# Hymba-style layer on one core: the small score and gate products move behind the near scores, in quadrants

## The reference, cut to what matters

```
proj = rmsnorm(x) @ w_in            # 1024 x 3072: sb q, k, v, gate; lru x, gate; xa q, gate
SB : stick-breaking attention, 8 heads x 64, strictly causal
     w = sigmoid(z) * prod of (1 - sigmoid(z)) over the later keys; out = w @ v
LRU: xc = width-4 causal convolution of lru_x
     r, i = sigmoid(xc_block @ w_rg + b_rg), sigmoid(xc_block @ w_ig + b_ig)   # 4 blocks of 64
     h = scan(exp(-8 r softplus(-lam)), sqrt(1 - a^2) * i * xc)
XA : softmax attention, 4 heads x 64, into 256 memory tokens
out = x + concat(sb*silu(gate), h*silu(gate), xa*silu(gate)) @ w_out
```

## Time and profile before

| | us |
|---|---|
| median of 3 runs (1554.22 to 1555.98) | 1555.12 |
| span of the profiled execution | 1551.8 |
| the runs' median over the span | 3.3 |
| TensorE busy | 1506.0 (97%) |
| VectorE busy | 1040.6 (67%) |
| ScalarE busy | 878.3 (57%) |
| GpSimd busy | 318.3 (21%) |

### The profile page before, as it was taken

One profiled execution on the slowest core, in us unless ns is written; L12 is line 12 of the kernel. 1 busy time (PEld: TensorE's weight loads), 2 busy tenths in 40 slices (PEclk: granted clock), 3 DMA queues, 4 the chain that ended last, 5 costly groups with the idle time before them and its releaser, 6 DMA issues.

```text
span 1551.8 us, 29770 instructions
## 1 busy us (share of the span) xinstructions
PE 1506.0 (97%) x10764; PEld 732.2 (47%) x10764; DVE 1040.6 (67%) x1907; ACT 878.3 (57%) x1593; POOL 318.3 (21%) x305
## 2 busy tenths in 40 slices
PE   4999999999999999999999999999999999999996
PEld 2444444444444444444444444444444444444452
DVE  6988766676666676666666665667666667666674
ACT  6887555565446565445566445566545556544661
POOL 3222111222211222212222211222211122221120
PEclk9999999999999999999999999999999999999998
DMA  9545665545655545555545556454555454565645
GB/s 364 197 126 103 155 131 111 118 115 133 145 124 120 119 116 126 142 122 128 130 105 122 138 125 145 109 117 114 134 140 131 115 118 116 128 145 123 124 95 137
DMA packets 443336, 205.83 MB, mean 133 GB/s; under 512 B 412000, under 2 KB 412448, under 8 KB 442144
## 3 DMA queue, kind: packets, MB, share of 16 engines
q1 hardware_dynamic: 443008, 205.18, 54.8%
q10 hardware_dynamic: 288, 0.13, 0.0%
HBM read 55.53 MB, written 50.53 MB: 68 GB/s over the span
## 4 chain that ended last, share of the span: by engine, by line
PE 85%; SPq 2%; ACT 2%; DMA 1%; issue 1%; DVE 1%; ACTq 0%; DVEq 0%
PE bank L1816 26%; PE bank L1818 25%; PE bank L1817 25%; PE bank L1900 2%; SPq L495 2%; PE bank L2014 2%; PE bank L1864 2%; PE bank L1885 1%; PE bank L1909 1%; DMA x_lo<-x_t 0%; PE bank L1953 0%; PE bank L1948 0%; PE bank L1950 0%; PE bank L1949 0%; ACT fail_and_take L1047 0%
## 5 line engine op out<-in xcount | busy, mean ns | idle before, releaser
L1816 PE MATMUL bank<-w_pair,x_hi 128*128 128x512 f16 x1528 | 581.6, 381 | 9.4 <-DVE w_pair L1248 5.2
L1818 PE MATMUL bank<-w_pair,x_lo 128*128 128x512 f16 x1528 | 580.6, 380 | 0.0
L1817 PE MATMUL bank<-w_pair,x_hi 128*128 128x512 f16 x1528 | 580.5, 380 | 0.0
L1143 ACT ACTIVATE spare<-xy,columns 128x1024 f16<-128x1024 f32 x32 | 36.8, 1149 | 395.4 <-DVE columns L1674 395.4
L1816 PEld LDWEIGHTS bank<-w_pair,x_hi 128*128 128x128 f16 x1528 | 149.7, 98 | 183.4 <-issue 6.9
L1818 PEld LDWEIGHTS bank<-w_pair,x_lo 128*128 128x128 f16 x1528 | 149.8, 98 | 181.4 <-issue 1.9
L1817 PEld LDWEIGHTS bank<-w_pair,x_hi 128*128 128x128 f16 x1528 | 149.9, 98 | 166.8 <-issue 2.7
L1816 PE MATMUL bank<-wo_pair,y_hi 128*128 128x512 f16 x480 | 181.9, 379 | 0.8 <-issue 0.8
L752 POOL TENSOR_TENSOR fail_and_take<-fail_and_take,seen 128x512 f32<-128x512 f32 x32 | 42.5, 1327 | 680.9 <-ACT fail_and_take L904 680.9
L1817 PE MATMUL bank<-wo_pair,y_hi 128*128 128x512 f16 x480 | 181.9, 379 | 0.0
L1818 PE MATMUL bank<-wo_pair,y_lo 128*128 128x512 f16 x480 | 181.9, 379 | 0.0
(11 more groups left out here) (271 smaller groups left out, 2398.3 us busy)
## 6 DMA issues: line engine op xcount, KB each, us to landing
xy<-in_x SPq DMA_DIRECT2D x32, 512.0 KB, 3.6
spare<-in_x SPq DMA_DIRECT2D x31, 512.0 KB, 4.1
out<-spare SPq DMA_DIRECT2D x30, 512.0 KB, 2.9
gate_kept<-gate SPq DMA_DIRECT2D x32, 256.0 KB, 2.2
v_kept<-v_sb SPq DMA_DIRECT2D x32, 256.0 KB, 2.1
fail_and_take<-v_sb SPq DMA_DIRECT2D x64, 128.0 KB, 2.4
q_kept<-q_t SPq DMA_DIRECT2D x32, 256.0 KB, 3.9
k_kept<-k_t SPq DMA_DIRECT2D x32, 256.0 KB, 4.4
```

Source lines behind the costliest of these rows:

```text
L1143: act.activation(y_halves[:, 0, :], xy[:, :], ACT.Copy, scale=y_top[:, :]).then_inc(s["y_high"], 1)
L1816: pe.matmul(dst, hi[:, k, :], pair[:, 0, k, :], start=k == 0, stop=False)
L1817: pe.matmul(dst, hi[:, k, :], pair[:, 1, k, :], start=False, stop=False)
L1818: last = pe.matmul(dst, lo[:, k, :], pair[:, 0, k, :], start=False, stop=k == KD - 1)
```

## The change

Four edits in one.

- `memory_scores` runs as 24 matmuls on the four 64x64 quadrants, and `gate_products` as eight f32 matmuls on quadrants, without the zero blocks of the block-diagonal weight. Both are issued directly behind `near_scores`, ahead of project(1), in bodies 2 to 31; body 1 keeps the old place, and tile 31's own products keep theirs.
- The banks change: memory scores go to TURN, gate products to SMALL and HEADS. A wait for the near sigmoids falls away, and `heads` now waits for the gate sigmoids.
- The gate sigmoids become eight of 64 partitions in place of four of 128. On ScalarE the high half of the mixed rows and the gate sigmoids come behind the near sigmoids, and `weights_high` ahead of the memory queries.
- On VectorE the convolution goes ahead of the mixed rows' factor, which moves into the next body; `mix_low` comes behind the query sums, `stick` ahead of the key sums, and `weights_low` ahead of the memory queries' sums.

The diff, cut to its core:

```diff
+        def memory_banks(tile):
+            return SCORE if isinstance(tile, int) and tile == 0 else TURN
+        def gate_banks(d):
+            return (SMALL, HEADS) if d else SCORE
+        def other_half(odd):
+            return slice((1 - odd) * HD, (2 - odd) * HD)
...
@@ scalar
                 if B and not (after or early):
                     sigmoids(1)
+                if C and not (after or end):
+                    mix_high(2)
+                if B and not (after or early):
+                    gate_sigmoids(1)
...
+                if B and not (after or early):
+                    weights_high(1)
                 if A:
                     have(act, proj_done[2], n)
...
-                if B and not (after or early):
-                    weights_high(1)
-                    for g, (dst, bias) in enumerate(((rec_g, brg), (in_g, big))):
-                        for h in range(LH):
-                            at = (g * LH + h) * P
-                            last = act.activation(dst[:, h, :], (SCORE[0], SMALL)[d][:, at:at + P], ACT.Sigmoid,
-                                                  bias=bias[:, h:h + 1])
+                    for h in range(LH):
+                        for odd in range(2):
+                            r, to = slice(odd * HD, (odd + 1) * HD), other_half(odd)
+                            at = gate_banks(d)[odd]
+                            act.activation(rec_g[r, h, :], at[r, h * P:(h + 1) * P], ACT.Sigmoid, bias=brg[r, h:h + 1])
+                            last = act.activation(in_g[r, h, :], at[to, h * P:(h + 1) * P], ACT.Sigmoid,
+                                                  bias=big[to, h:h + 1])
...
@@ vector
                 elif B and not after:
                     convolution(1)
+                if C and not (after or end):
+                    mix_factor(2, p)
...
                 if A:
                     head_sums(s["q_read"], s["q_sum"], 0, HS)
+                if C and not (after or end):
+                    mix_low(2)
...
+                if B and not (after or early):
+                    stick(1)
                 if A:
                     head_sums(s["k_read"], s["k_sum"], HS, HS)
...
-                if B and not after:
+                if B and not (after or early):
+                    weights_low(1)
+                if early:
                     stick(1)
                 if A:
                     head_sums(s["xa_read"], s["xq_sum"], 2 * HS, HX)
                     silu(s["xa_read"], s["gate_x"], PROJ[0][:, HX * HD:GC], slice(D - HX * HD, D), G_XA)
-                if B and not after:
+                if early:
                     weights_low(1)
...
@@ tensor
                 def memory_scores(d):
-                    if d:
-                        have(pe, s["sig"], n - 1)
...
-                            for odd in range(2):
-                                r = slice(odd * HD, (odd + 1) * HD)
-                                last = pe.matmul((TURN, SCORE)[d][odd][:, c * NM:(c + 1) * NM], xq_t[r, a, c, :],
-                                                 mk_t[r, b, c, :], start=a + b == 0, stop=a == 1)
+                            for top in (0, HALF):
+                                for odd in range(2):
+                                    r = slice(odd * HD, (odd + 1) * HD)
+                                    last = pe.matmul(banks[odd][top:top + HALF, c * NM:(c + 1) * NM],
+                                                     xq_t[r, a, c, top:top + HALF], mk_t[r, b, c, :],
+                                                     start=a + b == 0, stop=a == 1)
...
                 def gate_products(d):
                     have(pe, s["conv"], n - d, TAPS)
-                    have(pe, s["y_mixed"], n - 2)
+                    have(pe, s["y_mixed"], n - 2, ahead_of_loop=True)
...
-                    for g, by_head in enumerate((rg_blocks, ig_blocks)):
-                        for h in range(LH):
-                            at = (g * LH + h) * P
-                            last = pe.matmul((SCORE[0], SMALL)[d][:, at:at + P], by_head[:, h, :], xc[:, h, :],
-                                             start=True, stop=True)
+                    for h in range(LH):
+                        for by_head, turn_over in ((rg_blocks, False), (ig_blocks, True)):
+                            for odd in range(2):
+                                r = slice(odd * HD, (odd + 1) * HD)
+                                to = other_half(odd) if turn_over else r
+                                last = pe.matmul(gate_banks(d)[odd][to, h * P:(h + 1) * P], by_head[r, h, r], xc[r, h, :],
+                                                 start=True, stop=True)
...
                 if B and not (after or early):
                     near_scores(1)
+                    memory_scores(1)
+                    gate_products(1)
                 project(1, [(s["v_read"], n - 1), (s["out_ready"], n - 3)])
...
-                if B and not after:
+                if early:
                     memory_scores(1)
                     gate_products(1)
                 project(3, [(s["k_read"], n)])
...
                     have_turned(pe, w_turned, n - 1)
+                    have(pe, s["gates_read"], n - 1)
```

More of the change, by code:

```diff
@@ L964, in probs_high, with gate_sigmoids, mix_high @@
                                    ).then_inc(s["p_high"], 1)
+                def gate_sigmoids(d):
+                    have(act, s["gates_done"], n - d)
+                    have(act, s["h_done"], n - d - 1)
+                    if isinstance(n, int) and n == 1:
+                        act.wait_ge(mv_made, 2)
+                    for h in range(LH):
[5 more added lines that the diff above has]
+                                                  bias=big[to, h:h + 1])
+                    last.then_inc(s["gates_read"], 1)
+                def mix_high(d):
+                    have(act, s["y_factor"], n - d)
+                    if after:
+                        act.wait_ge(late_y_high, 16)
+                        act.wait_ge(y_turned, LATE_LOW + 16)
+                    else:
+                        have_turned(act, y_turned, n - d - 1)
+                    if A:
+                        have(act, qk_turned, n - d + 1, 96)
+                    act.activation(y_halves[:, 0, :], xy[:, :], ACT.Copy, scale=y_top[:, :]).then_inc(s["y_high"], 1)
                 if B and not (after or early):
@@ L1046, in rates_and_exponentials @@
                     for h in range(HX):
-                        last = act.activation(probs[:, h, :], (TURN, SCORE)[d][h % 2][:, (h // 2) * NM:(h // 2 + 1) * NM],
+                        last = act.activation(probs[:, h, :], memory_banks(n - d)[h % 2][:, (h // 2) * NM:(h // 2 + 1) * NM],
                                               ACT.Exp, bias=neg_mx[:, h:h + 1], scale=near_scale[:, 1:2],
@@ L1050, in rates_and_exponentials @@
                     last.then_inc(s["p_done"], 1)
+                if early:
+                    gate_sigmoids(1)
+                    weights_high(1)
+                    out_sum(7, (1, 2))
                 if B and not after:
[L1053 to L1056, removed]
                     rates_and_exponentials(1)
@@ L1133, in body @@
                     chunk_high(6, 1)
[L1134 to L1143, removed]
+                if last_one or after:
+                    mix_high(1)
             act.wait_ge(ident_rows_made, 2)
@@ L1539, in score_maxima @@
                     for odd in range(2):
-                        last = dve.tensor_reduce(mx[:, odd::2], (TURN, SCORE)[d][odd][:, :].rearrange("p (h s) -> p h s", s=NM),
+                        last = dve.tensor_reduce(mx[:, odd::2], memory_banks(n - d)[odd][:, :].rearrange("p (h s) -> p h s", s=NM),
                                                  AX.X, ALU.max)
@@ L1658, in body @@
                                       ).then_inc(s["y_mixed"], 1)
[L1659 to L1673, removed]
-                    dve.tensor_scalar(y_top[:, :], y_inv[:, :], TOP, None, ALU.mult).then_inc(s["y_factor"], 1)
+                if last_one or after:
+                    mix_factor(1, q)
                 if early:
@@ L1680, in body @@
                     beta_of(0)
-                if B:
+                if last_one or after:
                     mix_low(1)
@@ L2122, in laid_out @@
         "per_partition": np.concatenate([columns(i["norm_g"][0]), columns(i["mem_g"][0]), taps] + [
-            columns(i[n][0]) for n in ("conv_b", "b_rg", "b_ig", "lru_lambda")] + [
+            columns(v) for v in (i["conv_b"][0], i["b_rg"][0], i["b_ig"][0].reshape(-1, 2, P // 2)[:, ::-1].reshape(-1),
+                                 i["lru_lambda"][0])] + [
             twice(i[n][0]) for n in ("sb_q_g", "sb_k_g", "xa_q_g", "xa_k_g")], axis=1),
```

37 lines of the change are left out of this document (25 added, 12 removed).

## The result

| | before | after |
|---|---|---|
| median, us | 1554.67 (1554.16 to 1555.98, 4 runs) | 1544.66 (1543.68 to 1546.73, 4 runs) |
| ratio, 95% interval | 1 | 0.9935 [0.9923, 0.9947] |
| span of the profiled execution, us | 1551.8 | 1542.8 |

The change is faster by 10.0 us, 0.65%. The forecast was 1560, slower by 0.3%; what came is the rival "gate products at four quadrants at once", put at 1542.

What follows compares the result with a forecast made beforehand. TensorE, busy for all of each 46.13 us loop body, was taken as the bound. Span 1551.8 + 1.0 (loop) + 3.8 (ends) = 1556.6, with 3.3 for the runs' median 1560 us; range 1541 to 1578, all but the long cases.

Steps and rivals of the forecast that it cites:

- gate products at four quadrants at once: Rival for the gate products in loop bodies: insertion 1.99 us, body -0.52, ends near +1, time 1542 us; chance 0.25.
- nine steps: Gate products on TensorE: only one matmul's second pass and the next one's first run together, 1.00 us.
- the lower end (0.44): Lower bound for the 16 gate passes on TensorE: four at a time, four rounds, 0.44 us.
- The freed power: GpSimd's power in loop bodies: with `weights_low` ahead of the memory sums it falls from 4.57 to 3.54 us.
- the chain of 11.24: From ScalarE's read of the memory queries to the end of `silu_lru`: 11.24 us, down from 12.27.
- the wait of 0.21 at project(5): TensorE in loop bodies: project(5) waits 0.21 us for `silu_lru`, release at 11.28 against 11.07 of cover.
- the covered convolution: VectorE's convolution, moved ahead of the factor, ends before the gate products begin: no wait, 1.8 us to spare.
- the covered ScalarE work: Mixed rows' high half, `weights_high` and eight gate sigmoids fit ahead of ScalarE's memory queries; `weights_high` has 1.3 us of cover.
- under 0.85 us: Gate products' time on TensorE below which the four-quadrant rival decides for faster.
- the ends: First and last bodies and last tile: together near +4 us, less 0.4 for bodies 3 and 30.
- Bodies 1 and 2: VectorE and ScalarE full of weight splitting there; 1.15 us more on ScalarE, estimated loss 1.5 us.
- The tail: Last tile: eight gate sigmoids cost 1.15 us more, and its products leave and enter a mode once more, 0.2.

Runs made afterwards that it cites:

- e2_by_quadrant: The changed kernel with the eight gate matmuls reordered so that both channel halves of a quadrant stand next to each other; 1548.20 us, ratio 0.9955.
- e3_weights_low_back: The changed kernel with `weights_low` back behind the memory queries' sums; 1578.45 us, ratio 1.0147.
- e4_gate_early: The changed kernel with `silu_lru` between the reciprocal and the last step of beta on VectorE; 1541.76 us, ratio 0.9919.
- e1_gates_full: The changed kernel with gate products in the old block-diagonal form and four sigmoids of 128 partitions, left in the new place; 1558.01 us, ratio 1.0016.
- e6_memory_rows: The changed kernel with memory scores in the old form, 12 matmuls of 64 rows by 128 columns, gates on quadrants; 1553.72 us, ratio 0.9991.
- e9_second_body_old: The changed kernel with bodies 1 and 2 in the old order, quadrant forms and loop kept; 1542.36 us, ratio 0.9924.

## Why the prediction was wrong

**The step that failed** is "the two passes of one matmul use the same quadrant and stand next to each other in the program, so the second waits for the first [...] That makes nine steps, 1.00 us". It was the choice inside bounds that held: 0.54 us measured with the way out of the quadrants, which the sum counts apart (0.09), so 0.45, the lower end (0.44). A second pass does follow its first by 0.11 us; what failed is that the rest of the program waits behind it. The near scores' rows showed quadrants at work together, and I ruled them out for f32 by an argument from program order for which no row stood; e2_by_quadrant makes that order worse and pays 0.07 us a body. By the prediction's own numbers its nine steps (1.00) were no better but 0.1 worse than the eight of before (0.90 without the change of mode). The Trainium skill, page "TensorEngine Tiling (Array Packing)", section "Key Properties", has tiles of the array load and multiply in parallel; here it holds for f32 as well (16 passes in 0.54 us).

**What held.** The rival with the same sum was right about size: insertion 1.99 (1.98 measured), body -0.52 (-0.60). The 0.08 between them is on ScalarE: it reads the memory queries 832.54 - 832.13 = 0.41 us after the start of the projection's last matmul, 0.49 before. The freed power (3.54, measured 3.53), the chain of 11.24 (11.23), the wait of 0.21 at project(5) and its reason, the covered convolution and the covered ScalarE work are all in the trace, and e3_weights_low_back and e4_gate_early priced two of them from the other side: without the freed power +1.08 us a body, without the wait -0.16. Because project(5)'s gate ends the chain, TensorE's gain counted only up to 0.6 of 0.75 us. Its condition for faster, gates "under 0.85 us", was met by 0.45. That rival's time came near (1542 against 1544.66) in part by luck: it gave the loop 13.5 us, which gained 16.3, and the ends a loss near 1, which it did not work out and which is 7.3.

**What was mis-sized.** The ends: +3.8 in the sum (1.15 + 0.2 + 1 + 1.5, without the 0.4 that the text takes off again), +7.3 measured. Bodies 1 and 2 had an estimate of 1.5, and what lies ahead of body 3 lost 5.7. I saw that ScalarE and VectorE are full there but added only the extra instructions; the trace shows pieces of the splitting that wait for the other engine's piece, so that a new order moves waits through them, and in after the clock falls behind the longest. Body 31 was put at 1 and lost 0.7. The tail was put at 1.35 and lost 2.6. Its first and last gate sigmoid in ScalarE's timeline, and the step that they hold:

```profile
1495.11 0.36 ACT L988 ACTIVATE rec_g<-bank,given 64x128 f32<-64x128 f32 x1 [1.48 <-PE bank L1938]
...
1497.74 0.36 ACT L989 ACTIVATE in_g<-bank,given 64x128 f32<-64x128 f32 x1
1498.13 0.40 ACT L1069 ACTIVATE tanh_l<-rec_g,columns 128x128 f32<-128x128 f32 x1
```

The eight take 3.0 us, 1.8 more than the 1.15 of before, because they start 0.37 apart; "twice 1.15" gave them 2.3. With the old gate form (e1_gates_full) the stretch behind the last near scores is 51.17 us in place of 52.61, so the form is worth 1.4 of the 2.6. The other 1.2 are in 16 matmuls of an output product (`out_high`) near the end, which wait for a DMA. Their windows, before and after:

```profile
1520.13:1525.12 4.99, 4.99 (x20) 1.89 (x22) 2.36 (x6) 0.00 (x0) 0.87 (x1) 0.72 1.05 159
1510.17:1516.35 6.18, 6.18 (x20) 2.16 (x22) 2.08 (x5) 0.00 (x0) 0.40 (x1) 0.58 0.98 220
```

The same work takes 6.18 us in place of 4.99, at a granted clock of 0.58 in place of 0.72. TensorE had stood idle for 8.9 us ahead of it, 7.0 in before; but in e1_gates_full it takes 6.49 after 6.9 us idle, so the sigmoids are not shown to be the reason.

**What stays open.** Body 2 differs by up to 2.6 us between profiles of kernels that treat it nearly alike (53.19 in after, 55.31 in e4_gate_early, 55.75 in e6_memory_rows). Most of it is the clock. Two windows of e4_gate_early:

```profile
150.00:155.00 5.00, 2.61 (x7) 0.97 (x8) 4.56 (x7) 4.98 (x13) 2.89 (x2) 0.65 0.48 30
155.00:160.00 5.00, 5.00 (x17) 1.93 (x16) 4.08 (x6) 4.98 (x13) 1.55 (x2) 0.67 0.39 80
```

After has 0.66 and 1.00 there. Matmuls at the 1.2 GHz level cost 1.35 us in body 2 of after, 2.9 in e4_gate_early and 3.4, in two stretches, in e6_memory_rows, so 1.6 and 2.0 us of the differences. What decides how often the clock falls stays open: in e9_second_body_old it is granted in full throughout body 2, though project(5) waits 2.9 us. Runs of one kernel also differ by 3 us or more, and each profile shows one execution.

## What to carry to other kernels

Keep a bound's two ends apart until a row speaks for one: a rule about overlap that no row shows is worth as little against a gain as for it. A smaller form and a new place can each be worthless or harmful alone (+2.9% and +0.27% here) and pay together, because the place gives cover to what the form makes longer on another engine. In bodies where two engines hand work to each other without a gap, cost a new order by its waits and not by its instructions.

## Not expected of the hardware

- f32 matmuls of two passes run on four quadrants at once: 16 passes of 128 columns in 0.54 us, against eight of the full array in 0.99. They begin in groups of four, 0.11 us apart. A worse order in the program cost 0.07 us a body.
- Sigmoids of 64 partitions that change between two banks and two halves start 0.37 us apart; two of 128 partitions in one bank take 0.63 together. Which of the differences separates them was not tried.
- A VectorE instruction with two inputs in SBUF, `weights_low`, held a GpSimd instruction of 0.21 us for 1.30, as it held the power in before.
- The granted clock was lower in some stretches at the ends behind waits of TensorE, but not behind each of them (2.9 us in body 2 of e9_second_body_old without one), and cost 1.35 to 3.4 us in body 2 of after, e4_gate_early and e6_memory_rows.
